# Two transformer blocks on one core: where the late modulation units and the turned token rows stand around the expert choice

## What is computed

```
for l in range(DEPTH):                      # DEPTH = 2
    h = h + hybrid_mixer(rmsnorm(h, norm_mix[l]), w_in[l], ..., w_out[l])
    h = h + expert_choice_ffn(rmsnorm(h, norm_ffn[l]), w_router[l],
                              w_expert_gate[l], w_expert_up[l], w_expert_down[l])

def expert_choice_ffn(h, w_router, w_gate, w_up, w_down):
    aff = softmax(h @ w_router)             # 256 tokens x 16 experts
    gate, idx = top_k(aff.T, 32)            # each expert takes 32 tokens
    xe = h[idx]
    ye = (silu(xe @ w_gate) * (xe @ w_up)) @ w_down
    return zeros_like(h).at[idx].add(gate * ye)
```

```
def adaln(cvec, w, b):
    m = silu(cvec) @ w + b                  # w: 1024 x 6144
    return split(m, 6)
```

## Time and profile before

| | us |
|---|---|
| median of 3 runs | 2124.45 |
| lowest and highest of them | 2123.13 and 2127.17 |
| the profiled execution's own time | 2125.11 |
| its span in the profile | 2123.0 |

### The profile page before, as it was taken

The page is one execution under the profiler, slowest core; times in us unless marked ns, Lnnn a source line. Parts: engine busy times, 40 slices in busy tenths (PEclk is TensorE's granted clock), DMA queues, the critical chain, the costliest instruction groups (busy, mean ns, idle before and its releaser), DMA issues.

```text
span 2123.0 us, 31497 instructions
## 1 busy us (share of the span) xinstructions
PE 1917.3 (90%) x13966; PEld 1171.1 (55%) x13966; DVE 641.3 (30%) x988; ACT 546.9 (26%) x856; POOL 0.2 (0%) x4
## 2 busy tenths in 40 slices
PE   9999998787878999998998989889999998889887
PEld 8988833131312898883333434349999744434443
DVE  4576500000000558650241111038668300000001
ACT  4466300000000447620210222034554211011102
POOL 0000000000000000000000000000000000000000
PEclk9999999999999999999999999999999999999999
DMA  9735999999999962599999999983426999999997
GB/s 359 267 128 181 393 416 427 428 427 428 428 428 421 373 235 105 208 390 414 428 424 419 417 424 420 428 346 131 166 101 237 405 427 428 428 427 428 427 428 302
DMA packets 123007, 748.18 MB, mean 352 GB/s; under 512 B 6288, under 2 KB 27152, under 8 KB 83344
## 3 DMA queue, kind: packets, MB, share of 16 engines
q1 hardware_dynamic: 122896, 746.52, 86.2%
HBM read 745.45 MB, written 1.05 MB: 352 GB/s over the span
## 4 chain that ended last, share of the span: by engine, by line
PE 57%; DMA 36%; DVE 3%; ACT 2%; issue 1%; SPq 0%; DVEq 0%; ACTq 0%
PE bank L878 13%; DMA ring<-w_expert_up 12%; DMA ring<-moe_w_up 11%; PE bank L969 10%; DMA ring<-w_expert_down 9%; PE bank L1022 9%; PE bank L881 5%; DMA ring<-w_expert_gate 4%; PE bank_pair L819 4%; PE bank_pair L822 2%; PE bank L1000 2%; PE bank L905 1%; PE bank L1189 1%; PE bank L839 1%; PE bank L1210 1%
## 5 line engine op out<-in xcount | busy, mean ns | idle before, releaser
L969 PE MATMUL bank<-ring,arena 128*32 128x512 f32 (+1 forms) x2848 | 489.7, 526 | 88.4 <-DMA ring<-w_expert_up 40.1
L969 PEld LDWEIGHTS bank<-ring,arena 128*32 128x32 f32 x2848 | 146.9, 110 | 397.4 <-issue 206.7
L1022 PE MATMUL bank<-ring,arena 128*32 128x512 f32 x1408 | 307.1, 610 | 44.6 <-DMA ring<-w_expert_down 36.7
L1022 PEld LDWEIGHTS bank<-ring,arena 128*32 128x32 f32 x1408 | 75.6, 112 | 253.2 <-issue 186.1
L1875 ACT ACTIVATE arena<-bank 128x512 f32<-128x512 f32 (+1 forms) x130 | 66.9, 542 | 452.4 <-PE bank L984 217.4
L2451 DVE TENSOR_TENSOR arena<-arena,bank 128x512 f32<-128x512 f32 x24 | 15.8, 686 | 549.9 <-PE bank L969 549.9
L878 PE MATMUL bank<-extra_parts,ring_parts 128*128 128x256 f32 x1024 | 169.5, 282 | 0.0
L878 PEld LDWEIGHTS bank<-extra_parts,ring_parts 128*128 128x128 f32 x1024 | 140.3, 188 | 6.7 <-ACT arena_parts L1875 2.7
L878 PE MATMUL bank<-ring_parts 128*128 128x256 f32 x672 | 127.3, 283 | 2.1 <-DVE ring_parts L2878 1.1
L969 PE MATMUL bank<-arena 128*32 128x256 f32 (+1 forms) x832 | 110.8, 441 | 8.9 <-DMA arena<-moe_w_gate 5.7
L819 PE MATMUL bank_pair<-extra_parts,arena_parts 128*128 128x512 f32 x320 | 109.7, 396 | 0.0
(11 more groups left out here) (389 smaller groups left out, 2353.8 us busy)
## 6 DMA issues: line engine op xcount, KB each, us to landing
ring<-w_expert_down SPq DMA_DIRECT2D x62, 2048.0 KB, 23.7
ring<-w_expert_gate SPq DMA_DIRECT2D x58, 2048.0 KB, 21.8
ring<-w_expert_up SPq DMA_DIRECT2D x54, 2048.0 KB, 25.6
ring<-w_in SPq DMA_DIRECT2D x32, 2048.0 KB, 13.5
ring<-moe_w_up SPq DMA_DIRECT2D x24, 2048.0 KB, 34.1
arena<-moe_w_gate SPq DMA_DIRECT2D x20, 2048.0 KB, 36.3
ring<-moe_w_down SPq DMA_DIRECT2D x20, 2048.0 KB, 33.7
ring<-ada_w SPq DMA_DIRECT2D x12, 2048.0 KB, 17.8
```

The source lines that it names most:

```text
L969: last = pe.matmul(to[own_rows(half, e)].rearrange("p (q c) -> p q c", c=own), x_slots[:, c, 32 * e:32 * e + 32], w[:, k, half], start=c = ...
L1022: last = pe.matmul(banks[4 + e // PAIRS][own_rows(half, e), :].rearrange("p (x d) -> p x d", x=2), hidT[:, e // PAIRS * own + f % own, own ...
```

## The change

On PE alone, in each layer of the first block:

- the late modulation units 3, 4 and 5 run behind `router_part(2)` and ahead of `router_part(3)`, and so ahead of the second norm's sums. Before, unit 3 stood between `router_part(3)` and the turning of the affinities, and units 4 and 5 behind that turning;
- all four `token_rows`, in the order 0, 2, 1, 3, run ahead of the affinities' turning. Before, one stood ahead of it and three behind it and behind units 4 and 5;
- behind the affinities' turning stand 22 new products that nobody reads, on bank 0, while DVE chooses.

Nothing changes on the other engines. Their instructions, and what each waits for, are the same.

```
                     if n > 4:
                         router_part(n - 5)
+                for n in range(ADA_HEAD, ADA_UNITS):
+                    ada_unit(n)
                 router_part(3)
-                ada_unit(ADA_HEAD)
-                token_rows(0)
+                for j in (0, 2, 1, 3):
+                    token_rows(j)
                 pe.wait_ge(dve_done, dve_at("aff", loops))
                 out = take(2, "dve", "aff rows")
                 for half in range(TH):
                     last = pe.transpose(out[0:EXPERTS, half * P:(half + 1) * P], aff[:, half, :], ident)
                 last.then_inc(pe_done, pe_p.mark("aff rows"))
-                for n in range(ADA_HEAD + 1, ADA_UNITS):
-                    ada_unit(n)
-                for j in (2, 1, 3):
-                    token_rows(j)
+                idle_products(take(0, "act", "router exp"), 22, ones)
                 pe.wait_ge(dve_done, dve_at("idx diag 0", loops))
```

## The result

The changed kernel takes **2141.44 us** (median of 5 runs, 2137.24 to 2144.08) against 2124.45 (5 runs, 2122.54 to 2127.17): 17.0 us between the medians. That is slower, as forecast, but 12.6 us above the forecast of 2128.8 and 9.4 above the end of the range. The profiled execution took 2141.62, its span is 2139.5 against 2123.0.

What follows compares the result with a forecast made beforehand. Transfers bound the tiles, hanging on unit 0's end and so on the affinities' turning. From 2125.11, copy delays of 1.8 and 1.55 less 1.2 absorbed, with the clock fallen in one layer, make +3.65: 2128.8 us, range 2125.0 to 2132.0.

Steps and rivals of the forecast that it cites:

- The work ahead of the copy: PE from router_part(2) to DVE's copy of the affinities: at full clock 1.8 us later in first layer, 1.55 in second.
- The clock in the turnings: Token-row turnings on PE: even chance per layer of a low clock, adding 1.5 us to the copy's delay.
- case "both": Clock fallen in both layers: 3.3 + 3.05 - 1.2 = 5.15 us, so 2130.3; chance 0.20.
- The queue absorbs 0.6: Transfers at unit 11's load: 0.6 us of the delay absorbed in each layer, bounds 0 and 1.7.
- Everything behind starts later by what is left: Weight stream, next layer and second block: all shifted by the delay that the transfers do not absorb.
- They cost nothing while the clock is high: The 22 filling products beside DVE's choice: 5.8 us, ending 0.4 before DVE's diagonal, no cost.
- In this execution they give nothing: Filling products ahead of gather and unit 0: no gain, since the clock was 1.00 there already.
- The hole in the queue as the only thing that counts: Rival: filling the transfers' first hole wins 1.9 us in first layer, 2.3 in second, giving 2120.9; chance 0.06.
- The delay is not absorbed: Denies the rival that queue reserve behind unit 11 absorbs up to 1.7 us per layer, giving 2125.1; chance 0.15.
- The filling products did not end last: Denies the rival that low clock makes them outlast DVE's choice: 2132.7 us, up to 2141; chance 0.09.
- The rule of the Trainium skill: Turnings behind the thin products would let the clock fall and stay low into the filling products; rival's chance 0.09.

Runs made afterwards that it cites:

- wide ones: Changed kernel with six 128x512 filling products per layer in place of the 22 of 128x128: 2132.91 us, and 2134.64 when repeated.
- three traces of the old order: Kernel before, order around the choice untouched, with 176, 256 or 88 instructions of idle products in later tiles: 2130.23, 2126.24 and 2128.13 us.
- first padded kernel: Changed kernel with 10 more idle products per layer in a later tile, 256 instructions in all: 2140.61 us; the same kernel repeated: 2139.65.

## Why the prediction missed, step by step

- **The work ahead of the copy** was sized right: 5.45, 1.50 and 1.04 us for the estimates 5.5, 1.45 and 0.96. The copy came 4.0 us later, of which 0.85 had been there since 90 us, so 3.1 for the forecast 3.3 with the clock fallen. In the second layer it was 4.3 for 3.05; the 1.35 us wait on issue is about the difference. In the three traces of the order without narrow products it was 1.7 (forecast 1.8 with the clock high) and 2.1 to 2.5 (forecast 1.55 to 3.05).
- **The clock in the turnings**, taken as even, fell in both layers in the first profiled execution (16 records in 3.6 and 3.3 us), the prediction's case "both". Over all seven traces of the new order it fell in every second layer (2.6 to 3.7 us) and in two of the first (1.94 or 1.95 us in the other five).
- **"The queue absorbs 0.6"**: measured 0.4 and 0.1 by the first part of unit 11's load, within the bounds. **"Everything behind starts later by what is left"** fails: at 284 to 291 the half clock added some 1.2 us in one execution and nothing in the other. I had no term for the clock behind the gather.
- **"They cost nothing while the clock is high"** is the step that failed most. The products hid beside DVE, as said (5.08 us, 1.36 before the spreading). But I priced them as time on an engine and not as 176 instructions of code. The term was nothing; by the medians the products made the kernel 6.0 us slower than the same order without them, and 6.8 to 8.5 slower than wide ones. In the traces they cost 4.5 to 4.8 us in a loop 1500 us later, and a wait of 1.35 to 1.6 us in the second choice with a low clock behind it, 1.8 to 4.1 us at the copy. No rival had this, and the page showed the queue of instructions with its 91 packets.
- **"In this execution they give nothing"** took the clock of the kernel before, where two units and three token rows lay beside the choice. The same change takes these away. In the kernel so emptied the clock is low over both gathers, and the order by itself costs 11 us (2135.46), not 4. That clock is only a part of the difference: in the traces it is 3.1 us in the first layer and 1.8 in the second, but with wide products, which take it away, the order still costs 8.6 and 9.8 us by the medians. The forecast with the clock fallen in both layers was 5.15. So the order was sized too low as well, by some 4 us; the three traces of the old order that reach the second choice 1.7 to 3.2 us earlier suggest that the one trace the sum was built on was late there, which would be a part of it.
- **The rivals.** The hole in the queue as the only thing that counts is refuted: the stream does hang on unit 0, though the early holes may bind as well. The delay is not absorbed. The filling products did not end last (PE idle 1.36 us behind them); that this rival's top figure of 2141 is the measured one is chance. The rule of the Trainium skill cited with it, TensorE: Matmul & The Clock Gate, Part 4: PE-mode transpose, that turnings don't count as work for the clock, was tied to that rival, with a chance of 0.09. In the changed kernel's first layer the clock fell in the turnings and was back at 1.00 in the filling products (44 in 5.08 us). In the other traces it reached into their start at most (5.93 us in the first padded kernel). And in five first layers 16 turnings ran at full clock behind the thin products (1.94 or 1.95 us), so turnings did not by themselves bring the low clock there.

By medians: forecast +4.4; the order without cover +11.3; the changed kernel +17.0. What is open: why the changed kernel's times do not fall by the loop's 4.5 us when its loop is clean, what the order costs beyond the two choices, and why the medians of the wide and the padded kernels stand 1.4 to 3.9 us above their best execution.

## What to carry to other kernels

Added instructions have two prices, time on the engine and code. If a long loop follows anywhere behind, look at the instruction queue's packets before and after, and prefer few large idle products to many small ones. Judge a filler by the kernel that the same change leaves, not by the profile before. And where a load waits on either of two releases, a gain at one may be worth nothing until the other is at least as early.

## What the runs showed of the hardware

- **Code is fetched in pieces, and their edges matter.** The packets of the instruction queue are 1.95 MB / 119 = 16.4 KB each. The loop ran without fetches at 0, 32 and 256 added instructions and with 27 at 88 and 176; at 48 one execution had none and another 9. When a turn fetches, it fetches 9 pieces, not just one that is over:

```profile
q8 instruction: 9, 0.15, 0.5%
```

(DMA of the changed kernel in one turn, 1880 to 2000 us.) The Trainium skill, Advanced Engine Details and Errata, in ISA Cache, gives TensorE 128 KB for code in pieces of 16 KB or 256 instructions. The traces agree with the size of the pieces, and with 256 instructions in one: the kernel before has 27932 records of products and weight loads, less three repeats of the loop's 1618 that were not fetched 23078, over 91 packets 254 each. A turn of the loop is some 810 products and as many weight loads (stretch of one turn, kernel before):

```profile
1764.15:1876.30 112.15, 99.55 (x810) 48.15 (x808) 8.63 (x23) 13.54 (x28) 0.00 (x0) 1.00 1.01 427
```

By these figures of the Trainium skill that is an estimated 6.3 pieces, so it touches seven or eight by where it begins, and eight is all that 128 KB hold. If one piece beyond the loop is fetched as well, seven fit and eight do not, and nine would be fetched in a turn, as was measured. That last step, and that each piece is then gone when its turn comes, is only argued.
- **A jump to code that has to be fetched** costs PE 4.4 to 5.0 us idle a time, once or twice per turn, and 6.1 in one case. What it costs the kernel is not the idle time: 28 us moved the end by 4.5 to 5.0 us, 14.3 us by 4.7, and the single 6.1 by 2.0. In straight code the fetches mostly do not show (none of the 91 packets before has an idle time above 1 us with it), and only now and then there is one of 1.2 to 2.1 us.
- **The clock after such a pause.** It was 0.56 of full in the mean over 1779.3 to 1791.0, a stretch that begins within the first of two stalls, 9.5 us of idle time in all, and goes on behind the second.

```profile
1779.30:1791.00 11.70, 5.31 (x40) 4.34 (x44) 0.00 (x0) 1.25 (x4) 0.00 (x0) 0.56 1.00 426
```
